# Multiplying the attention probabilities by the inverse row sum on VectorE instead of GpSimd, in a two-layer attention stack followed by a gated block

## The reference

```
sc = einsum('bqkgd,bskd->bkgqs', qb, kb) * scale (+ bias, mask)
p  = softmax(sc, axis=-1)            # sliding window: with a sink added to the row's sum
o  = einsum('bkgqs,bskd->bqkgd', p, vb)
...
gated = concatenate([ya * silu(ag), yb * silu(bg), yc * silu(cg), ym * silu(mg)])
return layer_norm(alpha * x + gated @ w_out)
```

## Time and profile before

| What | us |
|---|---|
| median of 3 runs | 3826.68 (3824.68 to 3828.99) |
| the profiled execution's own time | 3826.21 |
| its span, first to last instruction | 3824.4 |
| TensorE busy | 3491.3 |
| VectorE busy | 1536.1 |
| ScalarE busy | 995.3 |
| GpSimd busy | 1622.9 |
| multiplications at L834, 256 of them | 330.3 |

### The profile page before, as it was taken

How to read it: one execution, slowest core, us unless ns; L and a number is a source line. 1 busy time by engine, 2 the same in 40 slices (tenths; PEclk the granted TensorE clock), 3 DMA queues, 4 the chain that set the end, 5 groups by cost and what they waited for, 6 DMA issues and landing times. The chain is left out here.

```text
span 3824.4 us, 50012 instructions
## 1 busy us (share of the span) xinstructions
PE 3491.3 (91%) x20046; PEld 1793.2 (47%) x20364; DVE 1536.1 (40%) x2383; ACT 995.3 (26%) x1743; POOL 1622.9 (42%) x1048
## 2 busy tenths in 40 slices
PE   6998996998899699999997999999997979999999
PEld 3554652554564244444443554555544434444444
DVE  4154447135535733332115355545544463333200
ACT  2333322233331400000001445545444321000000
POOL 2444651344464333332323555565654443333322
PEclk9998998999999899999997999999999989999999
DMA  3100112101021011111112111110111111111112
GB/s 112 40 24 34 59 57 82 40 33 37 17 83 39 22 54 51 49 49 47 50 68 75 35 40 41 50 42 26 52 41 67 47 33 50 49 49 55 41 51 78
DMA packets 52885, 188.33 MB, mean 49 GB/s; under 512 B 6624, under 2 KB 7136, under 8 KB 52192
## 3 DMA queue, kind: packets, MB, share of 16 engines
q1 hardware_dynamic: 51408, 181.08, 13.7%
q10 hardware_dynamic: 1296, 4.72, 0.3%
HBM read 173.20 MB, written 12.58 MB: 49 GB/s over the span
## 5 line engine op out<-in xcount | busy, mean ns | idle before, releaser
L1008 PE MATMUL pair<-operand,panel_parts 128*128 128x512 f16 x2816 | 1080.6, 384 | 143.4 <-DVE operand L1815 65.6
L1010 PE MATMUL pair<-operand,panel_parts 128*128 128x512 f16 x2816 | 1077.5, 383 | 13.2 <-issue 1.3
L1009 PE MATMUL pair<-operand,panel_parts 128*128 128x512 bf16 x2584 | 988.8, 383 | 0.0
L803 POOL TENSOR_SCALAR panel_parts<-panel_raw 128x1024 f16<-128x1024 f32 (+3 forms) x287 | 293.2, 1022 | 1599.5 <-PE pair L1010 973.0
L804 POOL TENSOR_TENSOR panel_parts<-panel_raw,panel_parts 128x1024 bf16<-128x1024 f32 (+3 forms) x287 | 631.3, 2200 | 23.9
L1008 PE MATMUL pair<-arena,panel_parts 128*128 128x512 f16 (+1 forms) x1216 | 464.1, 382 | 57.5 <-DVE arena L1815 44.0
L1008 PEld LDWEIGHTS pair<-operand,panel_parts 128*128 128x128 f16 x2816 | 276.7, 98 | 509.8 <-issue 160.6
L834 POOL TENSOR_SCALAR arena<-arena,row_inv 128x256 f32<-128x256 f32 (+7 forms) x256 | 330.3, 1303 | 342.4 <-DVE row_inv L1877 342.0
L1010 PE MATMUL pair<-arena,panel_parts 128*128 128x512 f16 (+1 forms) x1216 | 462.7, 381 | 5.4 <-issue 1.1
L1010 PEld LDWEIGHTS pair<-operand,panel_parts 128*128 128x128 bf16 x2816 | 277.8, 99 | 339.8 <-issue 13.0
L1009 PE MATMUL pair<-arena,panel_parts 128*128 128x512 bf16 (+1 forms) x1130 | 429.2, 380 | 0.0
(11 more groups left out here) (214 smaller groups left out, 4318.9 us busy)
## 6 DMA issues: line engine op xcount, KB each, us to landing
panel_raw<-in_wgu SPq DMA_DIRECT2D x88, 512.0 KB, 3.2
panel_raw<-in_wl SPq DMA_DIRECT2D x58, 512.0 KB, 3.3
panel_raw<-in_wm SPq DMA_DIRECT2D x56, 512.0 KB, 3.2
panel_raw<-in_wdn SPq DMA_DIRECT2D x32, 512.0 KB, 3.2
residual_spill<-residual SPq DMA_DIRECT2D x16, 512.0 KB, 3.6
residual<-residual_spill SPq DMA_DIRECT2D x15, 512.0 KB, 6.2
panel_raw<-in_wl SPq DMA_DIRECT2D x18, 384.0 KB, 3.0
panel_raw<-in_wdn SPq DMA_DIRECT2D x16, 384.0 KB, 2.9
```

The source lines that it names most:

```text
L803: chained(nc.gpsimd.tensor_scalar(WP[:, s, 0, 0:cols], RAW[:, s, 0:cols], HI_MAX, -HI_MAX, ALU.min, ALU.max))
L1008: nc.tensor.matmul(out, stat[0], mov[0], start=first, stop=False)
L1009: nc.tensor.matmul(out, stat[0], mov[1], start=False, stop=False)
L1010: return nc.tensor.matmul(out, stat[1], mov[0], start=False, stop=last)
```

## The change

VectorE multiplies the probabilities by the inverse row sum, each group directly behind its reciprocal. The reciprocal is now followed by a wait of VectorE for its own result (`chained`), and the multiplications signal the semaphore on which the transposes wait, as GpSimd's did. GpSimd's function `scale` of the layers, its calls, and the semaphore between reciprocal and multiplication are gone; GpSimd only splits panels in the layers. The mixer of the second block keeps its own `scale` on GpSimd.

```
-        slot_inverse = sem("slot_inverse")
...
-            def scale(n, group):
-                _, s = SLOTS[n]
-                pool.wait_ge(slot_inverse, 2 * n + group + 1)
-                for u in s.groups[group]:
-                    p = probs_of(n, s, u)
-                    b = 4 * (n % 2) + u.i
-                    nc.gpsimd.tensor_scalar(p, p, RI[:, b:b + 1], None, ALU.mult).then_inc(slot_scaled, 1)
...
-                for g in range(2):
-                    scale(l * NSLOT, g)
...
-                        if s.n + 1 < NSLOT:
-                            if part == 1:
-                                scale(n + 1, 0)
-                                if LAYER_SLOTS[s.n + 1].branch != "b":
-                                    scale(n + 1, 1)
-                            if part == 3 and LAYER_SLOTS[s.n + 1].branch == "b":
-                                scale(n + 1, 1)
...
-                V_.reciprocal(RI[:, c], RS[:, c]).then_inc(slot_inverse, 1)
+                chained(V_.reciprocal(RI[:, c], RS[:, c]))
+                for u in units:
+                    p = probs_of(n, s, u)
+                    b = 4 * (n % 2) + u.i
+                    V_.tensor_scalar(p, p, RI[:, b:b + 1], None, ALU.mult).then_inc(slot_scaled, 1)
```

## The result

The changed kernel takes **3833.5 us** (median of 19 runs), the kernel before 3826.8 us there (20 runs): a ratio of 1.0016, 95% interval 1.0009 to 1.0023, or +6.7 us (3.4 to 8.8). By the bound of 0.2% that the prediction used this is no difference; the interval reaches past it at one end, but leaves out zero. The forecast was 3831, +4.6 us.

A forecast was written before the change was run, and what follows sets the result against it. TensorE was taken as the bound. Per layer C 2.1, A 0.8, B 0.3 and G -0.9 sum to +2.3 us, for two +4.6, giving 3831 us; 3828 to 3835 by its own bounds, 3823 to 3841 with rivals.

The forecast's parts named there:

- The bound, and what is hidden: Attention stretches of both layers: TensorE bounds; GpSimd's 330.3 us of multiplications were hidden; only VectorE's delays of TensorE count.
- A: Last a slot: two 640-column multiplications ahead of c's rotations, +1.0 us, less 0.2 from faster additions; +0.8 us per layer.
- b's cover: In b slots VectorE idles 1.37 us before the next row maximum, over the largest multiplication's 0.7 us, so it hides.
- The price of a multiplication: On VectorE, 163 ns plus 0.52 ns a column: about 0.30 us for 256 columns, 93 us in both layers.
- C: Four c slots per layer: second-group multiplications delay the copy behind the reciprocals, and TensorE, by 0.53 us each; +2.1 us.
- B: Passage from c to b: four multiplications ahead of b's rotations, 1.05 us, less 0.6 and 0.15 back; +0.3 us per layer.
- The upper bound: Highest price of a multiplication: the mask addition's rate, 0.42 us for 256 columns; +8.0 us for two layers.
- G: TensorE's one wait for GpSimd, at the transposes, goes because VectorE scales at once; -0.9 us per layer.
- VectorE beside GpSimd: Beside GpSimd's scaling an addition pair loses 0.2 us and copies a fifth; beside a panel subtraction a pair loses 1.7 us.
- Rival 2: New stretches of half clock on TensorE make the kernel slower; size and place not in the text given; chance 0.14.
- Rival 3: Multiplications wait for panel splits, 1.7 us each at three places per layer without slack: 10 us, 3841; chance 0.13.
- Rival 1: Multiplications wholly hidden at the three kinds of place without slack, only gains stay: 3.7 us, so 3823; chance 0.15.

The follow-up runs named there:

- e1: The changed kernel with the multiplications of the probabilities left out altogether, reciprocals kept; 3826.0 us, the time of the kernel before to 0.1 us.
- e2: The changed kernel, but GpSimd scales in the c slots and VectorE in a, b and m; 3825.7 us, -0.3 us against the kernel before.
- e3: The changed kernel with the c slots' second-group sum, reciprocal and multiplications issued behind the copy of turned probabilities; 3826.1 us.
- e4: The changed kernel with each multiplication preceded by a second one by 1.0, in place; 3871.2 us, +45 us against the kernel before.
- e8: The changed kernel with each multiplication by the constant 1.0 in place of the inverse row sum; 3829.0 us in one run.
- e9: The changed kernel itself, unedited, measured once more in a second comparison; +5.3 us against the kernel before.
- e5: The changed kernel, but VectorE scales in the c slots alone and GpSimd in a, b and m; +1.2 us against the kernel before.
- e10: Repeat of e5, VectorE scaling in the c slots alone and GpSimd elsewhere; +1.1 us against the kernel before.
- e11: The changed kernel with the last a slot's reciprocals and multiplications issued behind the rotations of c's queries and keys; +7.4 us against the kernel before.
- e12: The changed kernel with only the c slots' second-group multiplications each preceded by another by 1.0; 3848.4 us, 16.3 us over e9.
- e7: The kernel before, GpSimd scaling everywhere, with the c slots' second-group sum and reciprocal behind the copy of turned probabilities; 3820.8 us.

## Why the prediction was nearly right

- **The bound, and what is hidden.** Right. GpSimd's work was hidden (e1), a, b and m cost nothing but A (e2, by its waits), and the cost sits where something of VectorE stands ahead of TensorE's wait (e3). That b's cover was wide was said too lightly: it holds for one multiplication (e4).
- **The price of a multiplication.** The term that was mis-sized: 0.35 us for 256 columns, not 0.30. It was read from an instruction with constants, and one with a column of numbers takes 0.06 us more (e8). With it C is 4 x 0.64 and not 4 x 0.53, A's gross 1.2 and not 1.0, B's 1.31 and not 1.05. The upper bound, 0.42, held.
- **C.** Right in mechanism and place, 2.6 us for 2.1. (Three names are off by some slots, without harm to the sum: the earlier trace rows is the seventh of the eight c slots, the rotations of b at B stand in the fifth, and A's reciprocals are of the last a slot but one.)
- **A.** +1.0 for +0.8, **B** +0.6 for +0.3 in layer 0, with the returns (0.2; 0.7) as forecast from the rows. Doubling layer 0 was not quite right for B: the waits of layer 1 gave it about nothing in the first profile and 0.6 in e9, e5 and e10.
- **G failed.** "The next to be late there is nothing of VectorE's: -0.9 us" did not ask what would be late instead. ScalarE's copy ended 0.14 us ahead of the transposes in the trace of before too, and was the cause all along (e1). This step alone took 1.8 us from the forecast.
- **VectorE beside GpSimd.** The trace after agrees with the rows: GpSimd's scaling, once gone, gave back 0.14 us a copy (824 to 685 ns) and 0.2 us a pair of additions (1.59 to 1.41 us). Beside the subtraction L803 VectorE lost far more: e4's multiplication of 768 columns, 0.62 us when no split is beside it, started 0.36 us behind the start of the subtraction and ended 0.42 us after its end.
- **Rival 2, the clock,** a slower kernel by new stretches of half clock, was at work, in the direction that was not considered. Layer 0's stretch of half clock behind 290 us is gone in after, e5, e9 and e10 (a clock of 1.00 from 285 to 310), all with the values' waits at 1.79 us, while before, e1 and e2 have it (0.86). It isn't simply the length of the waits: e3 with 0.81 us has lost it too (1.00), and e8 (waits of 1.67 us, clock 0.86), e11 (1.79 us, 0.80) and e12 (2.45 us, 0.80) have it. And it can go the other way: in e12 the c slots of layer 0 ran at 0.85 against e9's 0.90, which by the rate above took some 3.7 us.
- **Rival 3, collisions:** some 20 multiplications were stretched, and no place of C, A or B among them; e4 shows how near one in b is. **Rival 1,** wholly hidden: false.

The forecast of +4.6 stood so near to +5.3 and +6.7 because two errors met: the places came to 8.4 us by layer 0, 3.8 more than forecast (C, A and B 2.0, G 1.8), and some 2 to 3 did not reach the median. So the places were foreseen, and the nearness of the number is luck. That the clock takes something back in more than a few executions is supported by e5 and e10, whose mean clock over 11 executions each is 0.9674 and 0.9675, against 0.9663 and 0.9665 of the kernel before beside them. For the changed kernel itself it is weaker: e9's mean is 0.9668 against 0.9665, and how much of its 2 to 3 us is the clock's share and how much the draw of the parts outside the slots is not shown. What decides where a stretch falls stays open.

## What to carry to other kernels

Where a producer's last step (here a copy) waits behind work that nobody needs yet, look at the order of the two before moving work to another engine: putting the copy first gained 5.8 us with GpSimd's scaling (e7) and 7.4 with VectorE's (e3 against the changed kernel of the first comparison), and moving the work cost 5.3 to 6.7. Before counting a wait as gone, look for the second last thing that ends there. And where TensorE's granted clock moves between two levels, 1.00 and 0.50 here, the sum of waits is a forecast with an error of several us in either direction (e5 took 1.2 us over before where the places sum to 5.8, e12 16.3 over e9 where they sum to 6.4), so compare the granted clock of the stretches before explaining a difference of that size.

## What the runs showed of the hardware

- VectorE's multiplication by a column of per-partition numbers takes 0.06 us longer than by a constant when no split is beside it, at every width here: 353 and 293 ns for 256 columns, 753 and 693 for 1024 (e4's profile has both side by side).
- VectorE loses unequally beside two of GpSimd's operations: beside a scaling in place 0.2 us per pair of additions (1.59 us instead of 1.41), beside the subtraction L803 nearly all of the time that it still ran (2.37 us instead of 0.62 in e4, with 1.95 us of the subtraction left).
- A stretch of 6.8 us at a granted clock of 0.50 cost 2.8 us, less than half its length (3.4); TensorE was busy for 5.76 of the 6.80 us and waited for the rest.
- Half-clock stretches come and go between kernels that differ by 0.6 us in TensorE's waits, and between executions of one kernel: a mean clock of 0.86, 0.91 and 0.84 in the c slots of layer 0 in before, after and e11, and 0.85 and 0.89 in those of layer 1 in the changed kernel's two profiles.
